# Activations in two tiles of 512 columns, and weight copies tied to the event that uses them

## The reference

```
# block 1 (16 meta tokens are put ahead of the sequence)
h = rms_norm(h_res); q1,q2,k1,k2,v,u = split(h @ w_in)
o = diff_attention(rope(q1,q2,k1,k2), v); o = rms_norm(o)
y = gelu(s5_ssm(u)); y = rms_norm(y * sigmoid(y @ w_glu + b_glu))
h_res += rms_norm(concat(o, y) @ w_out)
h = rms_norm(h_res)
h_res += rms_norm((silu(h @ w_gate) * (h @ w_up)) @ w_down)
# block 2
h = rms_norm(x); proj = h @ w_in
mixed = concat(head_norm(retention(q,k,v)) * silu(gate), rwkv7_mix(proj[2048:]))
x += mixed @ w_o
x += (silu(hf @ w_gate) * (hf @ w_up)) @ w_down        # hf = rms_norm(x)
x += (p @ w_ple_up) * sigmoid(hp @ w_ple_gate)          # hp = rms_norm(x)
return rms_norm(x)
```

## Time and profile before

| | us |
|---|---|
| median of 3 runs | 3389.66 |
| lowest and highest | 3388.50, 3397.58 |
| profiled execution, its own time | 3409.39 |
| span of its trace | 3407.6 |
| mean granted TensorE clock, as a share of full | 0.943 |
| busy: PE, DVE, ACT, POOL | 91%, 44%, 36%, 36% |

### The profile page before, as it was taken

The page is one execution under the profiler, slowest core; times in us unless marked ns, Lnnn a source line. Parts: engine busy times, 40 slices in busy tenths (PEclk is TensorE's granted clock), DMA queues, the critical chain, the costliest instruction groups (busy, mean ns, idle before and its releaser), DMA issues.

```text
span 3407.6 us, 48139 instructions
## 1 busy us (share of the span) xinstructions
PE 3105.6 (91%) x19536; PEld 2396.3 (70%) x19536; DVE 1506.9 (44%) x2264; ACT 1225.1 (36%) x1969; POOL 1232.6 (36%) x698
## 2 busy tenths in 40 slices
PE   6997877898998889989999989998999989899997
PEld 4775655676766666877777767777777767788875
DVE  5844542443443461355555553435455554222233
ACT  3111214533432463243444344343434443322232
POOL 5811302132322323434444332434444432344432
PEclk9887888899999889999999999999999989999998
DMA  4343323222212254332222243332222222322231
GB/s 152 118 119 94 104 78 106 87 74 87 69 62 71 77 187 152 103 99 86 75 76 84 72 155 133 129 103 81 84 74 86 78 72 82 123 93 96 90 105 56
DMA packets 158030, 330.02 MB, mean 97 GB/s; under 512 B 34960, under 2 KB 74064, under 8 KB 157808
## 3 DMA queue, kind: packets, MB, share of 16 engines
q1 hardware_dynamic: 58752, 213.94, 18.8%
q10 hardware_dynamic: 99056, 112.99, 10.2%
HBM read 281.89 MB, written 44.97 MB: 96 GB/s over the span
## 4 chain that ended last, share of the span: by engine, by line
PE 79%; DVE 12%; ACT 3%; ACTq 2%; issue 2%; DMA 1%; POOL 0%; DVEq 0%; POOLq 0%
PE ps L1855 34%; PE ps L1896 13%; PE ps L1884 12%; PE ps L1706 2%; PE ps L1617 2%; DVE acc_dense L2291 2%; PE ps L1587 1%; DVE ffh_lo L2971 1%; PE ps L2090 1%; ACTq L988 1%; PE ps L1627 1%; DVE act_lo L2291 1%; PE ps L1734 1%; PE ps L1794 1%; PE ps L1982 1%
## 5 line engine op out<-in xcount | busy, mean ns | idle before, releaser
L586 POOL TENSOR_TENSOR w_lo<-w_raw,w_hi 128x1024 fp32r<-128x1024 f32 x408 | 999.5, 2460 | 1735.1 <-ACT w_hi L697 1731.4
L1855 PE MATMUL ps<-act_hi,w_hi 128*128 128x512 f32 x1696 | 701.5, 414 | 13.6 <-ACT qk_raw L697 8.1
L1855 PE MATMUL ps<-act_lo,w_hi 128*128 128x512 f32 x1696 | 677.2, 399 | 0.0
L1855 PE MATMUL ps<-act_hi,w_lo 128*128 128x512 f32 x1696 | 673.6, 397 | 0.0
L697 ACT ACTIVATE w_hi<-w_raw 128x1024 fp32r<-128x1024 f32 x378 | 390.2, 1052 | 152.8 <-DMA w_raw<-weights 75.2
L1855 PEld LDWEIGHTS ps<-act_hi,w_hi 128*128 128x128 f32 x1696 | 322.5, 190 | 108.4 <-issue 16.6
L1855 PEld LDWEIGHTS ps<-act_hi,w_lo 128*128 128x128 f32 x1696 | 323.0, 190 | 74.6
L1855 PEld LDWEIGHTS ps<-act_lo,w_hi 128*128 128x128 f32 x1696 | 322.5, 190 | 66.7 <-issue 1.7
L1884 PE MATMUL ps<-w_hi,ffh_hi 128*128 128x512 f32 x704 | 297.2, 422 | 60.8 <-DVE acc_dense L2291 57.4
L2291 DVE TENSOR_TENSOR acc_dense<-acc_dense,ps 128x512 f32<-128x512 f32 x352 | 242.1, 688 | 228.5 <-PE ps L1884 182.3
L1896 PE MATMUL ps<-w_hi,act_hi 128*128 128x512 f32 x640 | 261.5, 409 | 26.7 <-POOL w_lo L586 11.9
(11 more groups left out here) (372 smaller groups left out, 4284.7 us busy)
## 6 DMA issues: line engine op xcount, KB each, us to landing
w_raw<-weights SPq DMA_DIRECT2D x408, 512.0 KB, 3.5
rw<-rw_t ACTq DMA_DIRECT2D x24, 256.0 KB, 2.3
rw<-lora_t ACTq DMA_DIRECT2D x24, 256.0 KB, 2.0
row<-x ACTq DMA_DIRECT2D x8, 512.0 KB, 3.7
...
```

The costliest lines, as they stand in the source:

```text
L586: pool.tensor_tensor(w_lo[:, s], raw, w_hi[:, s].bitcast(F32), SUB).then_inc(w_ready, 1)
L1855: mm = pe.matmul(out, ws[w][:, s, P * k:P * k + P], acts[a][:, k, x], start=(k, w, a) == (0, 0, 0), stop=(k, w, a) == (KT - 1, 1, 0))
```

## The change

Two things change.

First, the activations. The columns of meta tokens and of the first half, as the first norm and the projections of the near half use them, are now `near_hi` and `near_lo`, [128, 8, 528], pitch 2112 bytes. All later work uses `act_hi_0`, `act_hi_1`, `act_lo_0`, `act_lo_1`, [128, 8, 512] each, pitch 2048 bytes. The tiles of half 0 lie over the near ones, those of half 1 behind them (where the first norm puts the second half's columns too), all within the bytes that `act_hi` and `act_lo` took. Their rows start 128 bytes past a multiple of 256; before, a row `k` began 4160 bytes after the one before, and its first token's column 64 bytes further in.

Second, the number of units to be made after an event. `W_BEHIND` goes from 4 to 3, and `weights_by` replaces the formula: the units that the next event begins, or, if that is more, the least of what is begun within six events (`W_LOOK`), three past what is begun now, and what slots allow, counted after the next event's ends. The order of units, the events and `FILLS` stay.

```
-    act_hi = place("act_hi", [P, KT, L], F32R, AT_ACT)
-    act_lo = place("act_lo", [P, KT, L], F32R, AT_ACT + KT * L * 4)
+    near_acts, half_acts = [], ([], [])
+    for n, name in enumerate(("hi", "lo")):
+        at = AT_ACT + n * KT * L * 4
+        near_acts.append(place(f"near_{name}", [P, KT, NEAR], F32R, at))
+        for h in range(2):
+            half_acts[h].append(place(f"act_{name}_{h}", [P, KT, BANK], F32R, at + h * KT * NEAR * 4))
+
+    def of_tile(part, ks, i):
+
+        return half_acts[i // HALF][part][:, ks, P * (i % HALF):P * (i % HALF) + P]
+
+    def first_cols(part, ks, c0, rows):
+
+        if c0 < NEAR:
+            return near_acts[part][:, ks, c0:c0 + rows]
+        return half_acts[1][part][:, ks, c0 - NEAR:c0 - NEAR + rows]
...
-    W_START, W_AHEAD, W_BEHIND = len(ORDER), 3, 4
-    EVENTS, ended, made_ready = {}, [W_START] * W_BEHIND, [W_START + W_AHEAD]
+    W_START, W_AHEAD, W_BEHIND, W_LOOK = len(ORDER), 3, 3, 6
+    EVENTS, begun, ended = {}, [], [W_START] * W_BEHIND
 
     def event(side, h, starts, ends):
 
         ORDER.extend((h, u) for u in starts)
-        assert len(ORDER) <= made_ready[-1]
+        begun.append(len(ORDER))
         ended.append(ended[-1] + len(ends))
-        made_ready.append(min(len(ORDER) + W_AHEAD, ended[-W_BEHIND] + SLOTS))
-        return side, made_ready[-1]
+        return side, len(begun) - 1
+
+    def weights_by(e):
+
+        soon = begun[min(e + W_LOOK, len(begun) - 1)]
+        return max(begun[min(e + 1, len(begun) - 1)], min(soon, begun[e] + W_AHEAD, ended[e + 1] + SLOTS))
...
+    assert all(weights_by(e) <= ended[e + W_BEHIND] + SLOTS for e in range(len(begun)))
+    EVENTS = {phase: [(side, weights_by(e)) for side, e in events] for phase, events in EVENTS.items()}
...
-                    mm = pe.matmul(out, ws[w][:, s, P * k:P * k + P], acts[a][:, k, x], start=(k, w, a) == (0, 0, 0), stop=(k, w, a) == (KT - 1, 1, 0))
+                    mm = pe.matmul(out, ws[w][:, s, P * k:P * k + P], half_acts[h][a][:, k, :], start=(k, w, a) == (0, 0, 0), stop=(k, w, a) == (KT - 1, 1, 0))
...
-                token_product(AT[h, U_OUT + 4 * j + uu], k, uu, acts, tok_cols(HALF * h + k), (0, 3, 0), mix_psum)
+                token_product(AT[h, U_OUT + 4 * j + uu], k, uu, half_acts[h], slice(P * k, P * k + P), (0, 3, 0), mix_psum)
```

More of the change, by code:

```diff
@@ L144, in build @@
     PASSES = ((0, 0), (0, 1), (1, 0))
-    acts, ws = (act_hi, act_lo), (w_hi, w_lo)
+    ws = (w_hi, w_lo)
     def tiles_of(c):
@@ L935, in output_high @@
                 act.wait_ge(o_turned, HEAD_UNITS * h + u + 1)
-                give(fn(act_hi[:, 2 * pair + hh, tok_cols(qi)], ps[:, 7, VD:2 * VD], ACT.Copy), o_hi)
+                give(fn(of_tile(0, 2 * pair + hh, qi), ps[:, 7, VD:2 * VD], ACT.Copy), o_hi)
             if h == 0:
@@ L1224, in ret_high @@
             act.wait_ge(ret_turned, i + 1)
-            give(fn(act_hi[:, 0:4, tok_cols(i)], ps[:, 6, :].rearrange("p (k n) -> p k n", k=4), ACT.Copy), ret_hi)
+            give(fn(of_tile(0, slice(0, 4), i), ps[:, 6, :].rearrange("p (k n) -> p k n", k=4), ACT.Copy), ret_hi)
         def mark(ins, sem, value):
@@ L1291, in rw_high @@
             act.wait_ge(rw_norm, nth("norm", "out", v))
-            give(fn(act_hi[:, 4 + 2 * s:6 + 2 * s, tok_cols(i)], yo[:, :, :], ACT.Copy), mix_hi)
+            give(fn(of_tile(0, slice(4 + 2 * s, 6 + 2 * s), i), yo[:, :, :], ACT.Copy), mix_hi)
         def rwkv(h):
@@ L1846, in first_dense, with dense_products @@
             yield from feed_forward(0, h)
-        def dense_products(pos, out, part, x, last):
+        def dense_products(pos, out, part, h, last):
             s = pos % SLOTS
@@ L2406, in output_low @@
             dve.wait_ge(o_hi, HEAD_UNITS * h + u + 1)
-            out = (slice(None), 2 * pair + hh, tok_cols(qi))
-            tt(act_lo[out], ps[:, 7, VD:2 * VD], act_hi[out].bitcast(F32), SUB, o_lo)
+            tt(of_tile(1, 2 * pair + hh, qi), ps[:, 7, VD:2 * VD], of_tile(0, 2 * pair + hh, qi).bitcast(F32), SUB, o_lo)
         def attention(h):
@@ L2680, in residual_half @@
                 if step >= 2:
-                    g, _, _, c0 = tiles[step - 2]
+                    g = tiles[step - 2][0]
                     take(hi_done)
                     for b in range(2):
-                        tt(act_lo[:, 4 * b:4 * b + 4, c0:c0 + P], ps[:, 4 + 2 * (g % 2) + b, :].rearrange("p (k n) -> p k n", k=4),
-                           act_hi[:, 4 * b:4 * b + 4, c0:c0 + P].bitcast(F32), SUB, act_ready if b else dve_step)
+                        where = (slice(4 * b, 4 * b + 4), HALF * h + step - 2)
+                        tt(of_tile(1, *where), ps[:, 4 + 2 * (g % 2) + b, :].rearrange("p (k n) -> p k n", k=4),
+                           of_tile(0, *where).bitcast(F32), SUB, act_ready if b else dve_step)
                 yield
@@ L2879, in rw_low @@
             take(mix_hi)
[L2880 to L2881 removed]
+            where = (slice(4 + 2 * s, 6 + 2 * s), i)
+            tt(of_tile(1, *where), yo[:, :, :], of_tile(0, *where).bitcast(F32), SUB, mix_lo)
         def rwkv(h):
```

61 lines of the change are left out of this document (27 added, 34 removed).

## The result

The changed kernel takes 3419.0 us in the median (3416.88 to 3419.14), the kernel before 3391.56 (3388.50 to 3397.58). The ratio is 1.0077, interval 1.006 to 1.0095: slower by 26 us. The profiled execution took 3416.88 us, 2 us under its median; that of before had taken 3409.39, 18 us over its own. Of these some 13 us lie ahead of phase 1: its first out product starts at 557.9 us before and at 545.1 now. That part scatters between executions, for it starts at 545.1 in e2_copies too, which has the old layout, and between 541.0 and 552.8 in the other runs. So I compare the traces from there on.

The account below looks back on a forecast made before the run. PE was taken as the bound, 91% busy with 79% of the chain, through matmul pace and waits. Layout -27 and copies +17 made -10 us on 3390, so 3380, with a range of 3352 to 3412.

Parts of the forecast that it names:

- the copies' term: ACT's weight copies and POOL's low parts come later, so PE waits: 32 us, net +17, bounds -5 to +32.
- The layout: L1855 and L1896 matmuls reading activations each give back 5.3 ns once rows start at 128: -27 us.
- My note on `k` 3 and 7: In L1855, rows of k=3 and 7 already start at 128, yet take 0.69 us, not L1884's 0.68.
- POOL's `w_lo` slip past one to three of its other steps: POOL makes the weights' low parts behind one to three more of its own steps; no separate cost given.
- The sum over places in ACT's order: 28 places where the low part comes after PE's first use, 32 us in all before relief and absorption.
- the first pair: First mixed pair of down units: both copies stand behind a silu, the second low part 1.2 us late.
- phase 4's start: Three units' copies behind `squares_last` rows and DMA issues; first low part 4.3 us late, 4.8 counted for all three.
- What is given back in phase 1: Relief elsewhere than at late places: ACT chains losing a copy, including PE's 12.13 us gap at 1115.80; 3 us.
- No loss of clock is added: At phase 4's start PE runs at half clock anyway, so its stalls were given no extra clock cost.
- as a whole: Prediction fails if PE's busy time falls by under 15 us or `acc_dense` waits grow by more than 10.
- the sign for the copies: PE's waits for POOL's `w_lo` grow from 11.9 us to 25 or more; wrong if they stay below 15.
- The rival that came true: Slower: layout under 7 us, late low parts at down pairs and phase 4's start cost 17 to 22; chance 0.24.

Follow-up runs that it names:

- e2_copies: Kernel before plus only the later copies, its activations left in one tile (old layout); 3438.5 us, ratio 1.0140 to the kernel before.
- e4_pool_late: Changed kernel with ACT's copies back in the old order, only POOL's `w_lo` late; 3402.8 us, ratio 1.0023 to the kernel before.
- e16_all: Changed kernel, both engines catching up ahead of all POOL's RWKV steps: POOL's order as before, ACT late elsewhere; 3395.5 us, ratio 1.0008 to the kernel before.

## Why the prediction was wrong

I forecast 3380, 10 us faster, as -27 + 17; measured is 3419, 26 us slower, as -22 + 48. The direction was wrong, and the copies' term is where it went wrong.

**The layout** came out at -22 (15 to 30) where I had -27, and the pace of the lines as I said, L1896 included, where I had doubts (397 to 389). The reason given holds in part: moving the tiles changes the pace, and by a little under half of what the layout gave. My note on `k` 3 and 7, that rows at 128 were still slower than the weights', was the sign of the rest: they gained too, from 690 ns to 680. (The tiles `near_hi` and `near_lo` have a pitch of 2112 bytes and not the old one, as I wrote; their pace stayed all the same.) The stationary operand shows the effect of the place too: in phase 2, where the retention's products have half 0 as stationary operand, PE's starts at L1908 lie 231.2 ns apart with its tiles at 192 and 227.0 with the layout alone. The Trainium skill ("TensorE: Matmul & The Clock Gate", "Step-by-step: what each phase is for") says that loading the next stationary operand takes nothing from the running matmul. These two figures do not agree with that in full, since only the place of the stationary operand differs between them. That page says nothing of where rows start; that place should change nothing was my inference from it, and the moved tiles refute it.

**The copies** were mis-sized: +17 forecast, +47 or 48 measured. Taking the step apart:

- "POOL's `w_lo` slip past one to three of its other steps", priced at nothing, is the step that failed. Alone, in e4_pool_late, it cost 30 us. 78 of them slip past 430 steps, 5.5 each. What had to be read is what those steps wait for, and the trace of before had it, in POOL's waits:

```profile
POOL kk L598 <- DMA aa<-rw: 41.7, 9, 10.3
```

  A `w_lo` put behind such a block inherits its wait and its 5.5 us. In the changed kernel these waits are 75.5 us, and seven stalls of PE (3.0 to 6.7 us, at 1524, 1561, 1841, 2334, 2371, 2437 and 2701 us; 33.5 us in all) stand behind one of the blocks. Letting `w_lo` pass them was worth 42 us.

```profile
POOL kk L616 <- DMA aa<-rw: 75.5, 10, 17.1
```

- The sum over places in ACT's order was good as a sum of waits. Forecast by phase: 9.9, 9.9, 7.4 and 4.8 us. Found, without the wait of 11.7 us that was there before: 9.4, 23.4, 30.7 and 6.3, and without the seven stalls 9.1 and 11.6 in phases 2 and 3. At the first pair 1.2 was forecast near 749 and 1.07 found; at phase 4's start 4.3 for the first unit and 4.25 found.

```profile
735.02 0.50 PE L1898 MATMUL ps<-w_hi,ffh_hi 128*128 128x512 f32 x1 [1.07 <-POOL w_lo L604]
...
2900.45 0.76 PE L1910 MATMUL ps<-w_hi,act_hi 128*128 128x512 f32 x1 [4.25 <-POOL w_lo L604]
```

- What is given back in phase 1 was under-rated. I counted 3 us for such places together; the 12.13 us gap of the earlier trace rows alone lost 9.6, and with that phase 1 broke even.
- "No loss of clock is added" is wrong at phase 4's start, where 3.4 us at half clock follow the second wait and the place costs 8 us for 6.3 us of waits. Six of the seven stalls in phases 2 and 3 are followed by matmuls at half clock too, as at 1841.76; that at 2437 is not. From phase 1 on PE idles 38.5 us more than in the layout alone (218.4 and 179.9 in the table), and the phases are 51 us longer (2852.9 and 2802.1). The 12 us between are PE's own busy time; up to 8 of them are the lower clock, which is granted for some 217 us of these phases and for 200 with the layout alone.
- ACT's place, for which I had 32 us of raw waits and 17 net, cost 25 with POOL's order kept (e16_all). POOL's 30 and ACT's 25 sum to 55 against the 48 of the whole, which is within the intervals.

My signs did not warn of this. PE's busy time fell by 35 us and the waits for `acc_dense` fell, so the forecast "as a whole" stood by them, and the sign for the copies (waits for `w_lo` of 25 us or more) had no upper end: 81.5 passed it.

**The rival that came true** is only in part the one I wrote. I had a slower kernel at 3407 to 3412 through a layout that gives less than 7 us, with copies at 17 to 22. The layout gave 22, and the copies cost twice the top of their range. 3419 is outside my range because the copies' upper bound came from ACT's queue alone, and the 8 us that I put on POOL and DVE meeting came from `ffh_lo`, not from POOL's waits. These had a price in the trace of before: nine waits for `aa`, 41.7 us, which as an estimate of the upper end would have taken the range past 3419.
